# Low-rank products in couples of opposite row halves, and the key sums of a pair read one place later, in the projection stage of a two-layer backbone

## Chip, cores, metric

The kernel runs on 1 core of one Trainium2 chip. The metric is device microseconds of one execution of the whole program.

## What is computed

Two DeepNorm layers on 1024 latent and 256 context tokens of width 1024. Layer 0 projects all 1280 tokens once (`e_w_in`) and feeds four gated-linear-attention heads and eight RWKV-7 heads; layer 1 is an mLSTM block. The change is in what stands between the projection and the RWKV scan. There, for each of the two directions:

```python
p = p + (quad_shift(p, grid[0], grid[1]) - p) * mu
r, k, v, g, wl_f, wl_b, al_f, al_b = split_cols(p, RWKV_SIZES)
kk = to_heads(k * k_k, RWKV_HEADS).astype(jnp.float32)
kk = kk * lax.rsqrt(jnp.maximum(jnp.sum(jnp.square(kk), -1, keepdims=True), 1e-24))
w = jnp.exp(-RWKV_DECAY_SCALE * jax.nn.sigmoid((w0 + jnp.tanh(w_lr) @ ww2).astype(jnp.float32)))
a = jax.nn.sigmoid(a0 + a_lr @ wa2)
kh = to_heads(k * (1.0 + (a - 1.0) * k_a), RWKV_HEADS)
bonus = jnp.sum(rh * kh * rk, -1, keepdims=True) * vh
```

`w_lr` and `a_lr` have rank 64 per direction, so `w_lr @ ww2` and `a_lr @ wa2` contract over 64 rows only.

## The kernel before

**The projection stage** (`project_phase`) makes 26 column tiles of 128 channels, numbered as in `TILES0`: tile 0 is `wl` (the decays' low-rank channels, forward direction in rows 0 to 63 and backward in 64 to 127), tile 1 is `al` (the same for `a`), then k, r, v, g of head pairs 0 to 3 in tiles 2 to 17, then the linear-attention tiles 18 to 25. Each tile's 1280 tokens are cut into three pieces, `PIECES`, of 512, 512 and 256 columns. `project_split` (lines 469 to 471) runs 24 TensorE (PE) matmuls for a piece, since weights and activations are each split into a high and a low part.

**What is interleaved.** Beside the projection, the stage prepares the RWKV scan pair by pair. Pair p starts at tile b = 5 + 5p, so pairs 0 to 3 start at tiles 5, 10, 15 and 20. The table `PREP_PE` says which small products PE runs after which piece of which tile:

- `w0`, `a0` (forward low-rank products, three pieces each) after pieces 0 and 1 of tile b; `w1`, `a1` (backward) after pieces 0 and 1 of tile b+1 (line 869);
- `ksum`, the head sums of squared keys, three pieces against a full-height 128x128 constant, after piece 2 of tile b+1 (line 872);
- `blk0` after piece 1 of tile b+4, `blk1` and `bonus` of the pair before after pieces 1 and 2 of tile b (lines 857 and 872).

All of these write to two PSUM banks, 6 and 7, in turn. The product with number x in that order may start only when the product x-2 has been read:

```python
x = PREP_SEQ.index((name, p, i))
return x, 6 + x % 2
```

and `bank_free(x)` waits for `by_act` (ScalarE, ACT, read it) or `by_dve` (VectorE, DVE, read it).

**The other engines** work through the tiles in order, each with a `prep(n)` for the pair ahead of its own work on tile n:

- ACT: `high(n+1)` (the next tile's weights, line 911), `prep(n)` (sigmoids at k = n - b of 0 and 1, line 927; logarithm, root and the six exponentials at k = 2, lines 950 to 952 and 935 to 940), eviction of tile n (line 966), then `post(n-1)`.
- DVE: `prep(n)`, then the seven `shift_op`s that mix tile n (lines 487 and 495) once ACT has evicted it. At k = 1: squares (1039, 1040), `decay(p, 0)` and `decay(p, 1)` (ten scans, line 1008, and a subtraction, 1010, each; each waits for the third piece of `a0` or `a1`), then the three pieces of `ksum` are read out of PSUM (line 1047). At k = 2: kk times the root (1050). At k = 3 and 4: the operands of the scan. At k = 0 of the next pair: `blocks(p-1, 1)` (line 1018), which first waits until SyncE (SP) has stored the blocks of the forward direction, then the bonus (1032).
- SP issues all DMAs of the stage in one queue: weights, stored tiles, the scan's operands (`put`, line 764), and the block products (`blocks_away`, eight transfers, line 771).
- GpSimd (POOL) makes the low part of each tile's weights (line 980).

Of the kernel before, what the change touches and what calls it, by code (L numbers as in the profile page):

```python
# [22 lines left out]
P = 128  # L23
# [7 lines left out]
CH = 128  # L31
NCH = T // CH
# [124 lines left out]
NPAIR = len(PAIR_PARAMS)  # L157
# [64 lines left out]
def front_program(nc, A, G, xnat, hi, lo, w, wlr, win, modw, modb, modrow, gates_sb, full, rows, c_rows, cols1):  # L222
# [6 lines left out]
    n_rows = NPAIR + 1 + 2 + 1 + 2 * TILE_PARAMS  # L229
    sems = ("consts x_in c_in c_ps rows_in zeroed modb_in w0 w1 w2 w3 mod_k cols cols_sb cond_sb mod_ps mod_row vec_ps vec_sb gates_ps gate_row "  # L230
            "gate_ps gate_sb stored w_in small_in turned taken hi_ok lo_dve lo_pool")
    with phase(nc, sems) as (block, s):
# [100 lines left out]
        def _(act):  # L333
# [10 lines left out]
            act.dma_start(rows[V_MULR:V_MULR + 2, 0, :],  # L344
                          A.p["rwkv_mu"][0, 2048:2304].rearrange("(i n) -> i n", n=P)).then_inc(s["rows_in"], 16)
# [176 lines left out]
PREP_PE = {}  # L522
for _p in range(4):
    _b = PREP_AT + PREP_TILES * _p
    PREP_PE[_b, 0], PREP_PE[_b, 1] = [("w0", _p)], [("a0", _p)] + ([("blk1", _p - 1)] if _p else [])
    PREP_PE[_b, 2] = [("bonus", _p - 1)] if _p else []
    PREP_PE[_b + 1, 0], PREP_PE[_b + 1, 1], PREP_PE[_b + 1, 2] = [("w1", _p)], [("a1", _p)], [("ksum", _p)]
    PREP_PE[_b + 4, 1] = [("blk0", _p)]
PREP_PE[PREP_AT + 4 * PREP_TILES, 1] = [("blk1", 3)]
PREP_PE[PREP_AT + 4 * PREP_TILES, 2] = [("bonus", 3)]  # L530
PREP_SEQ = [(name, p, i) for key in sorted(PREP_PE) for name, p in PREP_PE[key] for i in range(2 if name[0:3] == "blk" else 3)]
# [11 lines left out]
def values_phase(nc, A, G, hi, lo, free, win, w, wh, wl, wvh, wvl, wlr):  # L543
# [8 lines left out]
    with phase(nc, sems) as (block, s):  # L552
# [6 lines left out]
        def _(sp):  # L559
# [17 lines left out]
            for n in range(2):  # L577
                sp.wait_ge(s["hi_ok"], 2 + n)
                sp.wait_ge(s["lo_pool"], 2 + n)
                sp.dma_start(w[:, n], win[:, :, TILES0[n][2]:TILES0[n][2] + P]).then_inc(w_in[n], 16)  # L580
# [8 lines left out]
            for i in range(2):  # L589
                sp.wait_ge(v_out[i], 16 * (NCH // 2))  # L590
                sp.wait_ge(w_in[i], 32)
# [88 lines left out]
def project_phase(nc, A, G, xnat, hi, lo, LW, LA):  # L680

    win = A.p["e_w_in"][0].rearrange("(k p) n -> p k n", p=P)
    with ExitStack() as ctx:
# [41 lines left out]

        def job(n):
# [7 lines left out]
        with phase(nc, sems) as (block, s):  # L734
# [26 lines left out]
            def _(sp):  # L761
# [12 lines left out]
                def load_wab(p):  # L774
                    if p:
                        sp.wait_ge(s["pp_ps"], PREP_SEQ.index(("a1", p - 1, 2)) + 1)
                    for d in range(2):
                        for i, x in enumerate(("rwkv_ww2_", "rwkv_wa2_")):
                            sp.dma_start(wab[64 * d:64 * d + 64, i], A.p[x + "fb"[d]][0][:, p * P:(p + 1) * P]).then_inc(s["lr_in"], 16)
# [58 lines left out]
            def _(pe):  # L838
# [8 lines left out]
                def block_product(p, d):  # L847

                    ops = (aa[0], sg[0]) if d == 0 else (sg[1], kk)
                    for h in range(2):  # L850
                        x, bank = piece_of(f"blk{d}", p, h)
                        bank_free(x)
                        q = slice(64 * h, 64 * h + 64)
                        for c in range(NCH):
                            for k in range(4):
                                t = slice(c * CH + 32 * k, c * CH + 32 * k + 32)
# [2880 lines left out]
```

## Time and profile before

| | us |
|---|---|
| median of 3 runs (lowest, highest) | 2911.9 (2903.33, 2916.92) |
| the profiled execution, its own time | 2909.42 |
| its span | 2907.6 |
| PE busy, share of span | 2505.9, 86% |
| DVE, ACT, POOL busy | 1625.3, 918.4, 786.4 |
| mean granted clock of PE, as a share | 0.922 |

The profile is one execution. The span runs from its first to its last instruction; 1.8 us lie around it. The projection stage's tiles begin at 169.9 us and its last product starts at 640.2 us. PE is busy 86% of the span as a mean over stages of quite different kinds, so the share says little about this stage; it is read by its own windows below. In the timelines, neighbouring records of one line on one engine are merged into a row, and what stands in brackets is the idle time before the row and what ended it. An fp32 matmul leaves two records.

### The profile page before, as it was taken

To read this page: it belongs to the slowest core of one execution; us is meant where nothing else is said; L and a number is where in the kernel's file an instruction comes from. 1 tells how busy PE (TensorE), PEld (TensorE's weight loads), DVE (VectorE), ACT (ScalarE), POOL (GpSimd) and SP (SyncE) were. 2 spreads that over 40 slices of the span, in tenths; PEclk is the share of its full clock that TensorE was granted. 3 is DMA by queue.
4 is the path that set the end of the run, shared out by engine and by line. 5 is a ranking of instruction groups with operands and counts; after the bars stand their busy time and mean duration, and the time that the engine had idled before them with its cause. 6 is when DMAs were issued, how large, how long until landed. Compare 5 with 4: busy or idle time off the path is not lost. (4 is left out here: it accounts for less than half of the span.)

```text
span 2907.6 us, 56618 instructions
## 1 busy us (share of the span) xinstructions
PE 2505.9 (86%) x24270; PEld 2129.0 (73%) x24270; DVE 1625.3 (56%) x2534; ACT 918.4 (32%) x1488; POOL 786.4 (27%) x745
## 2 busy tenths in 40 slices
PE   6899999987989884675978999999699999996986
PEld 2577776666877873554766888788599999996865
DVE  3037787644555635883585665665545656564233
ACT  2113243321232235552213333333343434340311
POOL 1111111107666533120313222222222222121421
PEclk8899999997999985777988999999899999998998
DMA  7612445644424413121562444444624343412521
GB/s 270 241 52 85 138 135 147 194 144 146 125 66 124 121 46 92 48 57 41 182 127 86 155 164 161 166 153 151 241 99 164 109 160 125 145 59 77 201 91 60
DMA packets 338281, 374.11 MB, mean 129 GB/s; under 512 B 111279, under 2 KB 274742, under 8 KB 335470
## 3 DMA queue, kind: packets, MB, share of 16 engines
q1 hardware_dynamic: 337024, 367.15, 39.2%
q8 instruction: 192, 3.15, 0.4%
q10 hardware_dynamic: 1006, 3.33, 0.3%
q14 instruction: 59, 0.48, 0.1%
HBM read 230.60 MB, written 139.82 MB: 127 GB/s over the span
## 5 line engine op out<-in xcount | busy, mean ns | idle before, releaser
L3321 PE MATMUL PS<-V_hi,weights_hi 128*128 128x258 f32 x832 | 237.8, 286 | 10.4 <-DVE H L3532 6.9
L469 PE MATMUL PS<-hT_hi,w_in_hi 128*128 128x512 f32 (+1 forms) x640 | 239.6, 374 | 4.7 <-DVE q_out L3120 4.7
L3322 PE MATMUL PS<-V_lo,weights_hi 128*128 128x258 f32 x832 | 236.7, 285 | 0.0
L471 PE MATMUL PS<-hT_hi,w_in_lo 128*128 128x512 f32 (+1 forms) x640 | 236.4, 369 | 0.0
L470 PE MATMUL PS<-hT_lo,w_in_hi 128*128 128x512 f32 (+1 forms) x640 | 236.3, 369 | 0.0
L3323 PE MATMUL PS<-V_hi,weights_lo 128*128 128x258 f32 x832 | 235.8, 283 | 0.0
L469 PE MATMUL PS<-h_hi,w_in_hi 128*128 128x512 f32 (+1 forms) x624 | 230.2, 369 | 5.6 <-PEq L115 3.6
L3429 POOL TENSOR_TENSOR weights_lo<-weights,weights_hi 128x1664 fp32r<-128x1664 f32 x32 | 122.0, 3813 | 412.6 <-ACT weights_hi L3381 412.6
L470 PE MATMUL PS<-h_lo,w_in_hi 128*128 128x512 f32 (+1 forms) x624 | 225.9, 362 | 0.0
L471 PE MATMUL PS<-h_hi,w_in_lo 128*128 128x512 f32 (+1 forms) x624 | 225.6, 362 | 0.0
L3293 PE MATMUL PS<-Q_hi,K_hi 128*128 128x256 f32 x640 | 184.7, 289 | 29.2 <-DMA K_lo<-kl_d 13.9
L3294 PE MATMUL PS<-Q_lo,K_hi 128*128 128x256 f32 x640 | 183.8, 287 | 0.0
L3295 PE MATMUL PS<-Q_hi,K_lo 128*128 128x256 f32 x640 | 183.7, 287 | 0.0
L980 POOL TENSOR_TENSOR w_in_lo<-w_in,w_in_hi 128x1024 fp32r<-128x1024 f32 x25 | 65.2, 2607 | 411.3 <-ACT w_in_hi L911 411.3
L3108 DVE SCALAR_TENSOR_TENSOR xnew<-padl,tile_cols,xnew 128x1024 f32<-128x1024 f32 x128 | 168.5, 1317 | 3.4
L3321 PEld LDWEIGHTS PS<-V_hi,weights_hi 128*128 128x128 f32 x832 | 158.6, 191 | 11.3 <-issue 11.3
L3322 PEld LDWEIGHTS PS<-V_lo,weights_hi 128*128 128x128 f32 x832 | 159.3, 191 | 0.0
L3323 PEld LDWEIGHTS PS<-V_hi,weights_lo 128*128 128x128 f32 x832 | 159.1, 191 | 0.0
L3367 ACT ACTIVATE weights<-M_row,head_cols 128x128 f32<-128x128 f32 x352 | 112.1, 389 | 114.1 <-DVE diag_arg L3477 58.5
L3293 PEld LDWEIGHTS PS<-Q_hi,K_hi 128*128 128x128 f32 x640 | 125.5, 196 | 30.7 <-issue 30.7
L469 PEld LDWEIGHTS PS<-hT_hi,w_in_hi 128*128 128x128 f32 x640 | 121.2, 189 | 33.3 <-DVE q_out L3120 13.6
L469 PEld LDWEIGHTS PS<-h_hi,w_in_hi 128*128 128x128 f32 x624 | 122.0, 195 | 26.4 <-issue 9.3
(462 smaller groups left out, 6348.6 us busy)
## 6 DMA issues: line engine op xcount, KB each, us to landing
chunk_in<-in_d SPq DMA_DIRECT2D x40, 512.0 KB, 3.4
w_in<-in_e_w_in_dram SPq DMA_DIRECT2D x30, 512.0 KB, 5.2
xnew<-in_o_w_in_dram SPq DMA_DIRECT2D x30, 512.0 KB, 6.2
in_d<-xnat SPq DMA_DIRECT2D x20, 640.0 KB, 6.0
modw<-in_mod_w_dram SPq DMA_DIRECT2D x12, 1024.0 KB, 9.5
xnat<-in_mod_w_dram SPq DMA_DIRECT2D x8, 1536.0 KB, 7.3
v_d<-xnew SPq DMA_DIRECT2D x16, 640.0 KB, 3.0
kh_d<-k_hi SPq DMA_DIRECT2D x16, 640.0 KB, 2.9
```

The source lines that it names most:

```text
L469: pe.matmul(PS[:, bank + off // 512, 0:n], wh[:, k], hh[:, k, t], start=(k == 0), stop=False)
L470: pe.matmul(PS[:, bank + off // 512, 0:n], wh[:, k], hl[:, k, t], start=False, stop=False)
L471: last = pe.matmul(PS[:, bank + off // 512, 0:n], wl[:, k], hh[:, k, t], start=False, stop=(k == KT - 1))
L3108: ins = dve.scalar_tensor_tensor(lat, padl[:, a:a + ROWS, b:b + GRID_W], col[tap], lat, ALU.mult, ALU.add)
L3293: pe.matmul(out, kh, QH[:, m % 2, kt], start=(kt == 0), stop=False)
L3294: pe.matmul(out, kh, QL[:, m % 2, kt], start=False, stop=False)
L3295: last = pe.matmul(out, kl, QH[:, m % 2, kt], start=False, stop=(kt == 3))
L3321: pe.matmul(out, wh, VH[:, j, q], start=(j == seen[0]), stop=False)
L3322: pe.matmul(out, wh, VL[:, j, q], start=False, stop=False)
L3323: last = pe.matmul(out, wl, VH[:, j, q], start=False, stop=(j == seen[-1]))
L3367: last = act.activation(W[:, n % 2, slot(d, c, j)], arg, ACT.Exp, bias=cols[:, d, j, h, 0:1], scale=-1.0)
L3429: pool.tensor_tensor(WL[n % 2][:], W[:, n % 2], WH[n % 2][:].bitcast(F32), ALU.subtract).then_inc(s["w_lo"], 1)
```

## The change

It has three parts. First, the channels of tile 1 (`al`) are loaded with their two 64-column halves exchanged, and so are its mix coefficients in the parameter rows, and `wa2` lies in the other half too. So `w` and `a` of one direction contract over opposite halves of the rows. This costs one more weight DMA for tile 1 (SP) and two more small parameter DMAs at the start (ACT). Second, `w` and `a` of a direction are issued as couples, piece by piece: one couple after each piece of tile b (forward) and of tile b+1 (backward). Third, `ksum` moves from after piece 2 of tile b+1 to after piece 0 of tile b+2; DVE reads it at k = 2 instead of k = 1, and kk times the root moves from k = 2 to k = 3.

The diff's core:

```diff
 for _p in range(4):
     _b = PREP_AT + PREP_TILES * _p
-    PREP_PE[_b, 0], PREP_PE[_b, 1] = [("w0", _p)], [("a0", _p)] + ([("blk1", _p - 1)] if _p else [])
...
+    for _d in range(2):
+        for _i in range(3):
+            PREP_PE[_b + _d, _i] = [(f"w{_d}", _p, _i), (f"a{_d}", _p, _i)]
+    if _p:
+        PREP_PE[_b, 1] += prep_all("blk1", _p - 1)
+        PREP_PE[_b, 2] += prep_all("bonus", _p - 1)
+    PREP_PE[_b + 2, 0] = prep_all("ksum", _p)
+    PREP_PE[_b + 4, 1] = prep_all("blk0", _p)
...
+        def half_of(i, d):
+
+            return d if i == 0 else 1 - d
...
+                            q = 64 * half_of(i, d)
+                            sp.dma_start(wab[q:q + 64, i], A.p[x + "fb"[d]][0][:, p * P:(p + 1) * P]).then_inc(s["lr_in"], 16)
...
+                    if name[0] in "wa":
+                        j = "wa".index(name[0])
+                        at = 64 * half_of(j, int(name[1]))
+                        q = slice(at, at + 64)
+                        ins = pe.matmul(PS[:, bank, 0:m], wab[q, j], (LW, LA)[j][q, t], start=True, stop=True)
...
-                    for name, dst, j in ((f"w{d}", sg[d], J_W0 + d), (f"a{d}", aa[d], J_A0 + d)):
-                        for i in range(3):
+                    for i in range(3):
+                        t, m = pieces(i)
+                        for name, dst, j in ((f"w{d}", sg[d], J_W0 + d), (f"a{d}", aa[d], J_A0 + d)):
...
                         decay(p, 0)
                         decay(p, 1)
+                    if k == 2:
                         for i in range(3):
                             x, bank = piece_of("ksum", p, i)
                             t, m = pieces(i)
                             dve.wait_ge(s["pp_ps"], x + 1)
                             dve.tensor_scalar(khs[:, t], PS[:, bank, 0:m], 1e-24, None, ALU.max).then_inc(s["by_dve"], 1)
-                    if k == 2:
+                    if k == 3:
                         dve.wait_ge(s["root"], p + 1)
                         link(dve.tensor_tensor(kk, kk, khs, ALU.mult))
-                    if k == 3:
                         dve.wait_ge(s["r_in"], 16 * (p + 1))
```

**The order on PE**, before, at tile 10 (`a0` of pair 1, `blk1` of pair 0, then the projection's piece 2) and, after the dots, at the end of tile 11 (`ksum` of pair 1):

```order
L471 MATMUL PS<-h_hi,w_in_lo 128x512
L869 MATMUL PS<-LA,w_pair_lr 128x512 x2
L869 MATMUL PS<-LA,w_pair_lr 128x256
L857 MATMUL PS<-pair_bufs,xnat 32x32 x80
L469 MATMUL PS<-h_hi,w_in_hi 128x256
...
L471 MATMUL PS<-h_hi,w_in_lo 128x256
L872 MATMUL PS<-pair_bufs,cst_pair 128x512 x2
L872 MATMUL PS<-pair_bufs,cst_pair 128x256
L469 MATMUL PS<-h_hi,w_in_hi 128x512
```

and with the change, the same places and the start of tile 12. `LW` and `LA` are tiles 0 and 1, the low-rank activations; lines 471 to 473 are the projection now, 889 the low-rank products, 877 the block products, 891 `ksum` and `bonus`:

```order
L473 MATMUL PS<-h_hi,w_in_lo 128x512
L889 MATMUL PS<-LW,w_pair_lr 128x512
L889 MATMUL PS<-LA,w_pair_lr 128x512
L877 MATMUL PS<-pair_bufs,xnat 32x32 x80
L471 MATMUL PS<-h_hi,w_in_hi 128x256
...
L889 MATMUL PS<-LW,w_pair_lr 128x256
L889 MATMUL PS<-LA,w_pair_lr 128x256
L891 MATMUL PS<-pair_bufs,cst_pair 128x512 x2
L891 MATMUL PS<-pair_bufs,cst_pair 128x256
...
L473 MATMUL PS<-h_hi,w_in_lo 128x512
L891 MATMUL PS<-pair_bufs,cst_pair 128x512 x2
L891 MATMUL PS<-pair_bufs,cst_pair 128x256
L471 MATMUL PS<-h_hi,w_in_hi 128x512
```

A run of three products of one kind became couples of `LW` and `LA` of one piece; the bonus now has a couple ahead of it; and the head sums have a tile's first piece ahead of them, 24 projection matmuls of 512 columns.

**The order on DVE**, before, pair 1: scans of the two directions, head sums, mix of tile 11, kk times the root:

```order
L1008 SCALAR_TENSOR_TENSOR xnat<-cst,xnat 128x128 x10
L1010 TENSOR_TENSOR xnat<-xnat 128x1280
L1008 SCALAR_TENSOR_TENSOR xnat<-cst,xnat 128x128 x10
L1010 TENSOR_TENSOR xnat<-xnat 128x1280
L1047 TENSOR_SCALAR pair_bufs<-PS 128x512 x2
L1047 TENSOR_SCALAR pair_bufs<-PS 128x256
L487 TENSOR_SCALAR p_out<-xnat,mix_keep 128x1280
L495 SCALAR_TENSOR_TENSOR p_out<-xnat,mix_mus,p_out 128x16x63 x2
L495 SCALAR_TENSOR_TENSOR p_out<-xnat,mix_mus,p_out 128x960 x2
L495 SCALAR_TENSOR_TENSOR p_out<-xnat,mix_mus,p_out 128x255 x2
L1050 TENSOR_TENSOR pair_bufs<-pair_bufs 128x1280
```

and with the change (1029 scans, 1031 subtraction, 489 and 497 the mix, 1069 head sums, 1072 kk times the root):

```order
L1029 SCALAR_TENSOR_TENSOR xnat<-cst,xnat 128x128 x10
L1031 TENSOR_TENSOR xnat<-xnat 128x1280
L1029 SCALAR_TENSOR_TENSOR xnat<-cst,xnat 128x128 x10
L1031 TENSOR_TENSOR xnat<-xnat 128x1280
L489 TENSOR_SCALAR p_out<-xnat,mix_keep 128x1280
L497 SCALAR_TENSOR_TENSOR p_out<-xnat,mix_mus,p_out 128x16x63 x2
L497 SCALAR_TENSOR_TENSOR p_out<-xnat,mix_mus,p_out 128x960 x2
L497 SCALAR_TENSOR_TENSOR p_out<-xnat,mix_mus,p_out 128x255 x2
L1069 TENSOR_SCALAR pair_bufs<-PS 128x512 x2
L1069 TENSOR_SCALAR pair_bufs<-PS 128x256
L489 TENSOR_SCALAR p_out<-xnat,mix_keep 128x1280
```

The three reads of the head sums stood ahead of the seven mix operations of tile 11 and now stand behind them; kk times the root went from ahead of the mix of tile 12 to behind it.

## Rows read from the trace of the kernel before

**Rows 1.** The page: busy time of TensorE (busy us, share, instructions).
```profile
PE 2505.9 (86%) x24270; PEld 2129.0 (73%) x24270; DVE 1625.3 (56%) x2534; ACT 918.4 (32%) x1488; POOL 786.4 (27%) x745
```

**Rows 2.** Windows: PE, PEld, DVE, ACT, POOL busy us (x instructions), clock, DMA share.
```profile
338.20:435.50 97.30, 91.95 (x719) 70.64 (x718) 78.32 (x82) 37.56 (x40) 11.78 (x5) 0.96 0.47 138
435.50:531.90 96.40, 91.33 (x718) 69.79 (x717) 80.99 (x87) 35.72 (x39) 13.53 (x6) 0.96 0.52 151
```

**Rows 3.** Groups of PE's small products: xcount | busy us, mean ns | idle before.
```profile
L869 PE MATMUL PS<-LW,w_pair_lr 64*128 64x512 f32 x32 | 15.8, 615 | 0.0
...
L872 PE MATMUL PS<-pair_bufs,cst_pair 128*128 128x256 f32 x16 | 6.0, 457 | 5.7 <-DVE pair_bufs L1047 5.7
L869 PE MATMUL PS<-LW,w_pair_lr 64*128 64x256 f32 x16 | 5.7, 438 | 5.0 <-ACT xnat L927 5.0
```

**Rows 4.** Timeline of PE, pair 1: start us, length us, line, records [idle before].
```profile
371.37 0.70 PE L869 MATMUL PS<-LW,w_pair_lr 64*128 64x256 f32 x2 [1.26 <-ACT xnat L927]
...
384.78 1.88 PE L872 MATMUL PS<-pair_bufs,cst_pair 128*128 128x512 f32 x4
387.87 0.70 PE L872 MATMUL PS<-pair_bufs,cst_pair 128*128 128x256 f32 x2 [1.21 <-DVE pair_bufs L1047]
```

**Rows 5.** Timeline of PE, later stage: products that alternate between row halves.
```profile
805.18 2.06 PE L1284 MATMUL PS<-chunk_in 64*128 64x128 f32 x32
```

**Rows 6.** Timeline of DVE, pair 1: scans, head sums taken, mix of tile 11.
```profile
382.42 3.27 DVE L1008 TENSOR_TENSOR_SCAN xnat<-cst,xnat 128x128 f32<-128x128 f32 x10 [3.06 <-ACT xnat L927]
385.72 1.49 DVE L1010 TENSOR_TENSOR xnat<-xnat 128x1280 f32<-128x1280 f32 x1
387.13 1.28 DVE L1047 TENSOR_SCALAR pair_bufs<-PS 128x512 f32<-128x512 f32 x2
...
388.94 1.35 DVE L487 TENSOR_SCALAR p_out<-xnat,mix_keep 128x1280 f32<-128x1280 f32 x1
390.33 6.12 DVE L495 SCALAR_TENSOR_TENSOR p_out<-xnat,mix_mus,p_out 128x1008 f32<-128x1008 f32 x6
```

**Rows 7.** Timeline of ACT, pair 1: last sigmoids, eviction, logarithm, last exponential.
```profile
381.30 1.09 ACT L927 ACTIVATE xnat<-PS,vc 128x512 f32<-128x512 f32 x2 [0.17 <-PE PS L869]
384.98 1.24 ACT L966 ACTIVATE xnat<-PS 128x1280 f32<-128x1280 f32 x1 [2.59 <-PE PS L471]
...
389.06 1.28 ACT L950 ACTIVATE pair_bufs<-pair_bufs 128x1280 f32<-128x1280 f32 x1 [0.60 <-DVE pair_bufs L1047]
...
399.32 1.35 ACT L940 ACTIVATE xnat<-xnat,half 128x1280 f32<-128x1280 f32 x1
```

**Rows 8.** Windows, columns as in rows 2: granted clock after two waits.
```profile
328.00:334.90 6.90, 6.12 (x30) 5.96 (x31) 6.73 (x9) 0.35 (x1) 0.00 (x0) 0.51 0.58 173
345.10:348.50 3.40, 3.40 (x10) 2.63 (x9) 3.29 (x4) 0.00 (x0) 0.00 (x0) 0.50 1.11 327
```

**Rows 9.** Timeline of PE: end of a block product of pair 0.
```profile
328.78 0.32 PE L857 MATMUL PS<-xnat 64*32 64x32 f32 x4 [2.96 <-issue]
```

**Rows 10.** Timeline of DVE: block products of pairs 0, 1, 2 taken.
```profile
355.15 1.09 DVE L1018 TENSOR_TENSOR blocks_out<-PS,cst_pair 128x320 f32<-128x320 f32 x2 [3.25 <-PE PS L857]
...
457.32 0.89 DVE L1018 TENSOR_TENSOR blocks_out<-PS,cst_pair 128x320 f32<-128x320 f32 x2 [3.37 <-DMA blk_d<-blocks_out]
...
552.78 0.89 DVE L1018 TENSOR_TENSOR blocks_out<-PS,cst_pair 128x320 f32<-128x320 f32 x2 [15.89 <-DMA blk_d<-blocks_out]
```

**Rows 11.** Timeline of PE: bonus products of pairs 0, 1, 2.
```profile
360.14 2.57 PE L872 MATMUL PS<-pair_bufs,cst_pair 128*128 128x512 f32 x6
...
457.96 3.97 PE L872 MATMUL PS<-pair_bufs,cst_pair 128*128 128x512 f32 x6 [2.35 <-DVE blocks_out L1018]
...
554.16 2.57 PE L872 MATMUL PS<-pair_bufs,cst_pair 128*128 128x512 f32 x6
```

**Rows 12.** Timeline of ACT's DMA issues and of PE, start of the program.
```profile
29.54 1.29 ACTq L355 DMA_DIRECT2D param_rows<-in_ml_skip_dram  x2
...
41.49 0.36 PE L316 MATMUL PS<-cst,param_rows 59*128 59x59 f32 x1
```

More of the change, by code:

```diff
@@ L522, with prep_all @@
 PREP_PE = {}
+def prep_all(name, p):
+    return [(name, p, i) for i in range(2 if name[0:3] == "blk" else 3)]
 for _p in range(4):
     _b = PREP_AT + PREP_TILES * _p
-    PREP_PE[_b, 0], PREP_PE[_b, 1] = [("w0", _p)], [("a0", _p)] + ([("blk1", _p - 1)] if _p else [])
[L526 to L531, printed above, removed]
+    for _d in range(2):
[6 more added lines that the diff above has]
+    PREP_PE[_b + 4, 1] = prep_all("blk0", _p)
+PREP_PE[PREP_AT + 4 * PREP_TILES, 1] = prep_all("blk1", 3)
+PREP_PE[PREP_AT + 4 * PREP_TILES, 2] = prep_all("bonus", 3)
+PREP_SEQ = [x for key in sorted(PREP_PE) for x in PREP_PE[key]]
 BY_ACT = [x for x in PREP_SEQ if x[0][0] in "wa"]
@@ L845, in bank_free, with block_product @@
                             pe.wait_ge(s["by_dve"], BY_DVE.index(before) + 1)
-                def block_product(p, d):
+                def block_product(p, d, h):
                     ops = (aa[0], sg[0]) if d == 0 else (sg[1], kk)
[L850 to L856, printed above, removed]
-                                ins = pe.matmul(PS[32 * k:32 * k + 32, bank, 32 * c:32 * c + 32], ops[0][q, t], ops[1][q, t],
-                                                start=True, stop=True)
-                        ins.then_inc(s["pp_ps"], 1)
@@ L861, in prep_product @@
[L861 to L873 removed]
+                    x, bank = piece_of(f"blk{d}", p, h)
@@ new lines, in block_product, with prep_product @@
+                    bank_free(x)
+                    q = slice(64 * h, 64 * h + 64)
+                    for c in range(NCH):
+                        for k in range(4):
+                            t = slice(c * CH + 32 * k, c * CH + 32 * k + 32)
+                            ins = pe.matmul(PS[32 * k:32 * k + 32, bank, 32 * c:32 * c + 32], ops[0][q, t], ops[1][q, t],
+                                            start=True, stop=True)
+                    ins.then_inc(s["pp_ps"], 1)
+                def prep_product(name, p, i):
+                    x, bank = piece_of(name, p, i)
+                    t, m = pieces(i)
+                    bank_free(x)
+                    if name[0] in "wa":
[3 more added lines that the diff above has]
+                        ins = pe.matmul(PS[:, bank, 0:m], wab[q, j], (LW, LA)[j][q, t], start=True, stop=True)
+                    else:
+                        ins = pe.matmul(PS[:, bank, 0:m], G.c("heads"), khs[:, t], start=True, stop=True)
+                    ins.then_inc(s["pp_ps"], 1)
@@ L884, in _ @@
                             ins.then_inc(s["prod"], 1)
-                        for name, p in PREP_PE.get((n, i), []):
-                            if name == "w0":
+                        for name, p, j in PREP_PE.get((n, i), []):
+                            if name == "w0" and j == 0:
                                 pe.wait_ge(s["lr_in"], 64 * (p + 1))
```

47 lines of the change are left out of this document (21 added, 26 removed).

## Prediction

> **What bounds the kernel now.** I read the page first: TensorE (PE) is busy for 2505.9 us, 86% of the span [rows 1], but that is a mean over many stages. The windows of the projection stage decide. While pairs 1 and 2 are prepared, PE is busy for 91.95 of 97.30 and for 91.33 of 96.40 us, VectorE (DVE) for 78.32 and 80.99, ScalarE (ACT) for some 36, and the DMA engines are about half busy [rows 2]. So PE sets the pace, and DVE follows with only about 17% to spare: PE time saved is worth its full length only while DVE, and what DVE releases, keeps up. The third view is the groups of PE's small products with their idle time, and the last is the timeline of one pair on each engine. I take pair 1: tile 11 ends at 384.78 us, where its head sums start. I call that moment E.
>
> **Low-rank products (removed PE time).** They take PE 15.8 + 5.7 us for `w` and as much for `a`, 43 in all, and 5.0 us of waiting for ACT to read the first of three pieces [rows 3]; without the last records' tails this is 47 us. A record of 512 columns costs 0.43 us: four took 1.88 us, of which 0.17 is a tail [rows 4]. A product is two records, so three pieces are 2.15 us, and the sixteen runs of three are 34.4 us. The other 7.6 us (47 less 34.4 and 5.0) are openings, two per run (one after the projection, one after the bank wait), 0.24 us each. Do two products in opposite row halves overlap? Before, no low-rank pair does, so I bound it. From below: 32 records of 64 rows and 128 columns, alternating between halves, took 2.06 us with their tail [rows 5]; one after another they would take a quarter of 0.43 us each, 3.4 us. Without the 0.27 us tail they ran at 1.8 us, so nearly two at a time. From above: no overlap, if a couple is too short. The rows have the same shape and kind of instruction, so I take full overlap. Then a couple costs one product: 8 x 2.15 = 17.2 us, and 24 openings x 0.24 = 5.7 us. **47 becomes 23: -24 us.** The bank wait of 1.26 us [rows 4] goes, since ACT now has a whole piece of projection to read a couple.
>
> **Clock.** After three of those waits PE's granted clock fell to 0.50 for 3.4 us (1.2 instead of 2.4 GHz) [rows 8], which show one. Each costs half of that: **-5 us.**
>
> The Trainium skill (TensorEngine Tiling, Key Properties) says that a change of tiling mode drains the engine. It speaks against couples, which change the mode 24 times instead of 16. It gives no price. By the rows this is the 0.24 us opening, already in the sum.
>
> **Head sums of squared keys.** Three products go to two banks, so the third waits until DVE has read the first. Before, DVE read it ahead of the mix of tile 11, and PE waited for 1.21 us in pair 1 [rows 4], 5.7 us in all [rows 3]. Now the read stands behind that mix, which cannot start before tile 11 is finished and evicted. In pair 1, from E: last couple 0.6, its two sigmoids 0.9 (512 and 256 columns took 1.09 [rows 7]), so the second scans can begin at 1.5. Scans 3.3 and subtraction 1.4: 6.2. Meanwhile the eviction (1.24 [rows 7]) is over at 2.8. The mix ran from 388.94 to 396.45, 7.5 us [rows 6]: 13.8. Reading the first piece, 0.7: 14.5. PE, after couple (0.6), a piece of projection (5.6) and two head sums (1.9), wants the bank at 8.2. It waits for **6.3 us**. Pair 2 has a mixed tile in the same place: 6.3 again. In pair 0 DVE is further behind; I take 8.5. In pair 3 the tile there is not mixed, the read is done at 6.9, and there is no wait. Together 21 us in place of 5.7: **+15.5 us.** A weight operation of GpSimd that holds up one DVE operation would add up to 2 us each; scans that have begun earlier would take off 1.
>
> **Clock after these waits.** A wait of 2.96 us [rows 9] was followed by 6.9 us at a clock of 0.51 [rows 8], a loss of 3.4. The shortest low stretch costs 1.7. I take 2.6 for each of three waits, less 1.7 that pair 0 pays already: **+6 us**, bounds +3 and +9.
>
> **What is late next.** DVE's last read of the sums at E + 16 releases ACT's logarithm. From there to the end of the last exponential ACT took 11.6 us (389.06 to 400.67) [rows 7], and the eviction of tile 12 stands behind it, so it comes at E + 29. Before, nothing held it. PE, itself 8 us late, has finished that tile at E + 25. kk times the root (1.5 us) now precedes the operands of the scan. Together DVE runs 3 to 5 us later against PE; I take 3. At tile 10, 15 and 20 a new couple stands ahead of the bonus, in a bank that DVE frees by reading the block product. PE also gets there 4.7 us earlier than before (3.9 and 2.9 us of low-rank work become 2.1). The gap closes by 7.7 us. Before, DVE had read the first half-block 4.5 us ahead of PE's bonus in pair 0 and 0.9 ahead in pair 2, and PE waited 2.35 in pair 1 [rows 10, 11]. So the added waits are 3.2, 7.7 and 6.8: **+17.5 us**, bounds 0 and +25.
>
> **The rest, at nothing.** Two more parameter DMAs on ACT, 0.65 us each: the last was issued by 30.8 us and PE uses them at 41.49 [rows 12]; with more than 12 us gone from that gap they would count. One more weight DMA on SP's queue, tile 1, issued a tile ahead of its use. `load_wab` issues four transfers as before, and SP passes no new wait. The order of ACT's sigmoids changes, not their number.
>
> **Sum:** -24 - 5 + 15.5 + 6 + 17.5 = +10 us. The profiled execution took 2909.42 us, 2.5 below the median of 2911.9: **2919 us**, 0.25% above the median. A measurement can tell about 0.5% from no change, 14.6 us, so this counts as no change. Most of what the couples save is paid back in waits for DVE.
>
> **Rivals.**
>
> *DVE's chain takes over (slower).* DVE has 78 to 81 us of work per pair [rows 2]. Add its new idle time behind ACT's exponentials (13 us, E + 16 to E + 29) and the waits for block stores (3.4 in pair 1 [rows 10]), for the bonus and for sigmoids (8), and a pair takes 103 us or more against 96 to 97. The place is the couple ahead of the bonus; it decides once the block stores land over 10 us after PE wants the bank. For: the stores already set DVE's read in pairs 1 and 2 [rows 10]. Against: in pair 0 there are 4.5 us of slack. Three pairs with 8 more each instead of the 3.3 of my sum: 2933.
>
> *Records of a couple run in order (near no change, or slower).* `w` first record, `w` second, `a` first, `a` second: then only the middle two overlap, and a couple costs three records instead of two. That is 8 x (0.43 + 0.43 + 0.21) = 8.6 us more, some of it hidden by the waits: 2926. The rows of the alternating stream fit this as well, since in a long stream each record finds a partner.
>
> The Trainium skill (TensorE: Matmul & The Clock Gate, The mechanism) has matmuls start and end in strict program order. By that rule a couple would cost the three records, and the sum would be 2928. No row here has an isolated couple.
>
> *The couple ahead of the bonus does not wait (small gain).* DVE catches up, having idle time before the next pair: 2902. For: two of three pairs had slack.
>
> *Neither wait comes (faster).* The head sums are read in time, so the savings of 29 us stay: 2881. Against it is the order on DVE, where the read follows the mix of a tile that PE has just finished.
>
> **How the numbers follow.** Forecast 0.50, DVE's chain 0.20, in order 0.12, no wait at the couple 0.13, neither wait 0.05. The forecast's own bounds are 2908 to 2929. The range for 8 in 10 leaves out the gain and the far end of the slow rival: 2899 to 2937. Slower by over 0.5% (above 2926.5): nearly all of the chain rival, half of the in-order rival, a seventh of the forecast, 0.32. Faster by over 0.5% (below 2897.3): 0.06. The rest: 0.62.
>
> **What would show it.** Low-rank products busy for 17 to 23 us instead of 43, two records starting together in each couple (in order: three record times). PE's third head sum idle for 6 to 9 us in pairs 0, 1 and 2, ended by DVE's read, none in pair 3. The mix of tile 12 starting about E + 30. A wait of 3 to 8 us at the third couple of tiles 10, 15 and 20, ended by DVE's read of the block product. The forecast is wrong if the head sums' wait stays under 3 us, or if the stage before tile 5 or anything behind the projection changes by more than 3 us.

## The result, and the profile of the changed kernel

The changed kernel takes 2927.1 us (median of 6 runs) beside 2914.1 us for the kernel before (6 runs in the same set). The ratio is 1.0057, with a 95% interval of 1.0039 to 1.0074: slower, by about the half per cent that a measurement of this kernel can tell from no change. The profiled execution spans 2922.9 us, 15.3 more than the one of before.

**Where the 15.3 us are.** The next stage's first product starts at 659.26 us before and at 672.25 now: 13.0 us come from the projection stage, 2.3 from everything behind it. Within the stage I add up PE's time on the timeline, from the first record of a group to the first record of the next (a wait counts with the group ahead of it), until the last bonus:

| PE time in the stage, us | before | change | difference |
|---|---|---|---|
| projection, with the waits at its groups' ends | 382.5 | 390.5 | +8.0 |
| low-rank products | 47.0 | 28.7 | -18.3 |
| head sums and bonus | 23.0 | 43.7 | +20.7 |
| block products | 17.8 | 20.7 | +2.9 |
| sum | 470.3 | 483.6 | +13.3 |

The page (busy us, share, instructions) answers to [rows 1]: PE does the same number of instructions in 11 us less, and the span is longer.

```profile
PE 2494.7 (85%) x24270; PEld 2127.6 (73%) x24270; DVE 1626.1 (56%) x2534; ACT 916.4 (31%) x1488; POOL 792.4 (27%) x745
```

Windows from the first couple of tile 10 to that of tile 15, and on to that of tile 20 (columns as in [rows 2], which answer to them). A pair now takes 103 us instead of 96 to 97. PE is busy for 86 to 89 us of it, and DVE has its 78 to 82 us of work as before:

```profile
344.40:447.07 102.67, 86.15 (x717) 67.55 (x717) 82.33 (x84) 37.91 (x40) 14.55 (x6) 0.95 0.49 141
447.07:550.29 103.22, 89.46 (x716) 69.45 (x716) 77.98 (x82) 34.07 (x37) 14.18 (x5) 0.92 0.47 135
```

What PE waits for in the stage (us in total, times, longest). Before, these waits for DVE were 5.7 for head sums and 3.5 for block products; now they are 37:

```profile
PE PS L891 <- DVE pair_bufs L1069: 25.9, 4, 8.4
PE PS L889 <- DVE blocks_out L1039: 10.9, 4, 5.3
PE PS L877 <- issue: 8.0, 2, 5.1
...
PE PS L877 <- ACT xnat L948: 2.6, 3, 0.9
```

**The couple works.** Timeline of PE in pair 1 (start, length, line, records, idle before), beside [rows 4]. The first records of `w` and `a` start 0.01 us apart, and so do the second ones, 0.53 us later. The couple of 512 columns, from its first record to the projection's next one, takes 1.06 us, the couple of 256 columns 0.63:

```profile
375.67 0.69 PE L889 MATMUL PS<-LW,w_pair_lr 64*128 64x512 f32 x1
375.68 0.69 PE L889 MATMUL PS<-LA,w_pair_lr 64*128 64x512 f32 x1
376.21 0.59 PE L889 MATMUL PS<-LW,w_pair_lr 64*128 64x512 f32 x1
376.21 0.59 PE L889 MATMUL PS<-LA,w_pair_lr 64*128 64x512 f32 x1
...
386.01 1.88 PE L891 MATMUL PS<-pair_bufs,cst_pair 128*128 128x512 f32 x4
396.08 1.22 PE L891 MATMUL PS<-pair_bufs,cst_pair 128*128 128x256 f32 x2 [8.19 <-DVE pair_bufs L1069]
```

**The head sums wait.** Timeline of DVE in pair 1, beside [rows 6]. E, the end of tile 11, is at 379.80. The second scans begin at E + 1.6 and take 5.4 us instead of the usual 3.3. Then come the subtraction and the whole mix of tile 11, and only at 395.34 is the first piece read. PE had wanted that bank since 387.9. Behind the read DVE idles for 12.8 us, because ACT has the logarithm and six exponentials ahead of the eviction of tile 12:

```profile
381.40 5.42 DVE L1029 TENSOR_TENSOR_SCAN xnat<-cst,xnat 128x128 f32<-128x128 f32 x10 [1.31 <-ACT xnat L948]
386.86 1.49 DVE L1031 TENSOR_TENSOR xnat<-xnat 128x1280 f32<-128x1280 f32 x1
388.27 0.88 DVE L489 TENSOR_SCALAR p_out<-xnat,mix_keep 128x1280 f32<-128x1280 f32 x1
389.18 6.12 DVE L497 SCALAR_TENSOR_TENSOR p_out<-xnat,mix_mus,p_out 128x1008 f32<-128x1008 f32 x6
395.34 1.29 DVE L1069 TENSOR_SCALAR pair_bufs<-PS 128x512 f32<-128x512 f32 x2
...
410.55 0.89 DVE L489 TENSOR_SCALAR p_out<-xnat,mix_keep 128x1280 f32<-128x1280 f32 x1 [12.78 <-ACT xnat L987]
```

The timeline of ACT shows the same chain: logarithm at 397.80 (before: 389.06), eviction of tile 12 at 409.30.

```profile
397.80 1.27 ACT L971 ACTIVATE pair_bufs<-pair_bufs 128x1280 f32<-128x1280 f32 x1 [13.05 <-DVE pair_bufs L1069]
...
409.30 1.21 ACT L987 ACTIVATE xnat<-PS 128x1280 f32<-128x1280 f32 x1
```

The 2.1 us that the scans took longer coincide with one operation of GpSimd, on its timeline; the scan that started at 383.64 ended at 386.20. By the Trainium skill (GPSIMD Engine Reference, Specifications) GpSimd and VectorE contend for their memory interface when a VectorE instruction has two inputs there; the trace agrees.

```profile
383.52 2.39 POOL L1001 TENSOR_TENSOR w_in_lo<-w_in,w_in_hi 128x1024 fp32r<-128x1024 f32 x1 [15.19 <-ACT w_in_hi L932]
```

**The waits for block products.** On DVE, the reads of the two directions' block products in pair 1, and the second one of pair 2, answer to [rows 10]:

```profile
446.45 0.87 DVE L1039 TENSOR_TENSOR blocks_out<-PS,cst_pair 128x320 f32<-128x320 f32 x2
466.11 0.89 DVE L1039 TENSOR_TENSOR blocks_out<-PS,cst_pair 128x320 f32<-128x320 f32 x2 [3.54 <-DMA blk_d<-blocks_out]
...
568.28 0.89 DVE L1039 TENSOR_TENSOR blocks_out<-PS,cst_pair 128x320 f32<-128x320 f32 x2 [11.05 <-DMA blk_d<-blocks_out]
```

On PE the same two reads each end a wait, at the first couple of tile 15 (a place that my prediction did not have) and at the third, ahead of the bonus:

```profile
447.07 1.19 PE L889 MATMUL PS<-LW,w_pair_lr 64*128 64x512 f32 x1 [5.33 <-DVE blocks_out L1039]
...
457.56 1.57 PE L877 MATMUL PS<-pair_bufs,xnat 64*32 64x32 f32 x160 [0.86 <-ACT xnat L948]
466.65 0.79 PE L889 MATMUL PS<-LW,w_pair_lr 64*128 64x256 f32 x1 [4.46 <-DVE blocks_out L1039]
```

Of the 5.33 us at the first couple, 2.0 are GpSimd's again: the last DVE operation ahead of the read took 3.51 us instead of 1.49, while GpSimd worked from 442.26 to 445.18. Before, its operation began when that read was under way (436.52 and 436.27), and held up what came behind it.

```profile
443.01 3.51 DVE L1088 TENSOR_TENSOR pair_bufs<-pair_bufs,xnat 128x1280 f32<-128x1280 f32 x1
```

**The clock behind the head sums' waits.** Windows of the stretches at half clock that follow the waits in pairs 0, 1 and 2 (columns as in [rows 2]). They last 10.2, 6.8 and 6.8 us, and PE is busy for 6.2, 3.3 and 3.9 us of them:

```profile
286.80:297.00 10.20, 6.15 (x15) 4.81 (x16) 4.88 (x7) 4.40 (x4) 0.00 (x0) 0.50 0.38 116
392.60:399.40 6.80, 3.32 (x8) 2.65 (x9) 4.31 (x7) 1.58 (x2) 0.00 (x0) 0.50 0.49 148
501.80:508.60 6.80, 3.88 (x9) 3.12 (x10) 3.78 (x6) 2.14 (x2) 0.00 (x0) 0.50 0.56 171
```

### The profile page after: what moved, and what is told of

Read it like the earlier page. It is cut to its first block and busy times, and to the rows that moved or that the text cites. A ratio compares the mean times of both kernels' runs of the same rounds, so it can differ in the third digit from the quotient of the medians.

```text
span 2922.9 us, 56624 instructions
## 1 busy us (share of the span) xinstructions
PE 2494.7 (85%) x24270; PEld 2127.6 (73%) x24270; DVE 1626.1 (56%) x2534; ACT 916.4 (31%) x1488; POOL 792.4 (27%) x745
## 5 line engine op out<-in xcount | busy, mean ns | idle before, releaser
L3342 PE MATMUL PS<-V_hi,weights_hi 128*128 128x258 f32 x832 | 237.8, 286 | 10.4 <-DVE H L3553 6.9
```

What stands on the lines that cost most here:

```text
L3342: pe.matmul(out, wh, VH[:, j, q], start=(j == seen[0]), stop=False)
```

## The experiments

Theory A is that of the prediction: PE loses its time where DVE reads a bank late, first because the read of the head sums stands behind a mix, and then because ACT's logarithm follows that read. Theory B is the rival "DVE's chain takes over": DVE bounds the stage anyway, and a wait taken away in one place comes back in another. The ratios below are to the kernel before, run on the same chip in the same set; its median was 2915.6 us in the set of e1 to e4, 2911.7 in that of e5 to e8 and 2912.5 in that of e9b to e12b. So kernels of different sets are compared by ratio, and 0.1% is 3 us. "Stage" is the start of the next stage in the profiled execution (659.3 before), and "waits" what PE waits there for DVE.

| | us | ratio (95%) | stage | waits |
|---|---|---|---|---|
| the change | 2927.1 | 1.0057 (1.0039 to 1.0074) | 672.3 | 37.1 |
| e1, read ahead of the mix | 2902.4 | 0.9954 (0.9938 to 0.9969) | 653.0 | 18.0 |
| e2, couples alone | 2917.1 | 1.0012 (0.9999 to 1.0025) | 666.8 | 29.6 |
| e3, head sums' move alone | 2929.5 | 1.0050 (1.0033 to 1.0067) | 678.8 | 21.8 |
| e4, couples in one row half | 2938.2 | 1.0075 (1.0056 to 1.0093) | 686.8 | 32.1 |
| e5, e1 and root early | 2900.2 | 0.9962 (0.9949 to 0.9975) | 647.9 | 14.3 |
| e6, e1 and stores first | 2891.1 | 0.9937 (0.9921 to 0.9953) | 644.5 | 13.3 |
| e7, e1 and eviction between | 2892.1 | 0.9934 (0.9923 to 0.9946) | 640.8 | 11.8 |
| e8, e5, e6 and e7 together | 2888.0 | 0.9922 (0.9910 to 0.9934) | 636.2 | 7.3 |
| e9b, before, with the edits of e6 and e7 | 2907.8 | 0.9985 (0.9972 to 0.9998) | 657.0 | 5.7 |
| e10b, the change with them | 2919.5 | 1.0028 (1.0017 to 1.0039) | 669.1 | 30.6 |
| e11b, e12b in one row half | 2898.9 | 0.9958 (0.9946 to 0.9970) | 647.0 | 5.0 |
| e12b, e1 with them | 2888.9 | 0.9921 (0.9905 to 0.9938) | 637.5 | 8.3 |

### e1: the read ahead of the mix

```diff
                         decay(p, 1)
-                    if k == 2:
                         for i in range(3):
                             x, bank = piece_of("ksum", p, i)
```

> The change, but DVE reads the head sums ahead of the mix of tile b+1 (k = 1) instead of behind it; PE's place of the product (after piece 0 of tile b+2) and all else as in the change. Theory A (PE loses its time waiting for a read that stands behind the mix, and the later waits ahead of the bonus come from the same late read through ACT's logarithm): the third head sum waits for 1 to 1.5 us instead of 8.2 in pairs 0 to 2, ACT's logarithm starts some 8 us earlier against PE, DVE idles for under 8 us ahead of the mix of tile 12 instead of 12.8, and most of the 10.9 us of waits for the block products goes: 2927 less 21 less 4 to 10 = 2896 to 2902. Theory B (DVE's chain is the bound and the head sums' wait only shows it): the waits for block products grow by what the head sums' wait loses, and the time stays within 5 us of the change's, 2922 to 2932.

The time is 2902.4, 0.4 us above what theory A expects and 20 us from theory B. The timelines of PE and DVE in pair 1 show the third head sum waiting for 1.1 us instead of 8.2, and DVE idle ahead of the mix of tile 12 for 5.9 us instead of 12.8:

```profile
383.96 0.70 PE L891 MATMUL PS<-pair_bufs,cst_pair 128*128 128x256 f32 x2 [1.11 <-DVE pair_bufs L1068]
```
```profile
384.69 0.42 DVE L1068 TENSOR_SCALAR pair_bufs<-PS 128x256 f32<-128x256 f32 x1 [0.19 <-PE PS L891]
...
397.98 0.89 DVE L489 TENSOR_SCALAR p_out<-xnat,mix_keep 128x1280 f32<-128x1280 f32 x1 [5.91 <-ACT xnat L987]
```

So moving one read across one mix is worth 25 us by the medians and 1.0%, some 30 us, by the ratios; 19.3 us lie in the stage. What theory A has wrong is the rest: of 10.9 us of waits for block products 10.4 stayed (9.1 at couples and 1.3 at the last bonus), and 4.3 came up for operands at the block products of tiles 9, 14 and 19, where PE now arrives earlier than DVE is ready. So 22.6 us of waits for head sums went and 19.1 us of waits for DVE in all: a sixth came back, as theory B says of the whole. One thing e1 leaves open: it takes 6.9 us off DVE's idle time in pair 1 together with PE's wait, so it doesn't say how much of the gain came over either. e10b below takes time off DVE's idle time alone.

### e2: couples alone, e3: the move alone

```diff
-    PREP_PE[_b + 2, 0] = prep_all("ksum", _p)
+    PREP_PE[_b + 1, 2] += prep_all("ksum", _p)
```

with the read at k = 1 and kk times the root at k = 2, as before (e2). And, on the kernel before (e3), with the read at k = 2 and the root at k = 3:

```diff
-    PREP_PE[_b + 1, 0], PREP_PE[_b + 1, 1], PREP_PE[_b + 1, 2] = [("w1", _p)], [("a1", _p)], [("ksum", _p)]
+    PREP_PE[_b + 1, 0], PREP_PE[_b + 1, 1], PREP_PE[_b + 2, 0] = [("w1", _p)], [("a1", _p)], [("ksum", _p)]
```

> Parts one and two of the change alone: couples, with the head sums where they were before, after piece 2 of tile b+1 and read at k = 1. Theory A: the head sums now stand right behind a couple, whose backward scans (3.3 us and a subtraction of 1.5) stand ahead of their read on DVE, so the third sum waits for 4 to 6 us in all four pairs (before: 1.2), a little less in total than the 25.9 of the change; the read is some 7 us earlier than in the change, and the waits for block products shrink. About 2927 less 6 less 0 to 8: 2913 to 2921. Theory B (DVE's chain is the bound): within 5 us of the change. If moving the sums were what costs the couples their whole gain: 2927 less 20, 2907 or below.

> Part three of the change alone, on the kernel before: runs of three low-rank products as before, head sums after piece 0 of tile b+2 and read behind the mix of tile b+1. Theory A: a1 is done 2 us later against E than with couples, so the wait is the same or longer from there on: PE wants the bank at E + 7.6 and DVE reads at E + 9 to 11 in pairs 1 and 2 (E the end of tile b+1), a wait of 2 to 3.5 us instead of 1.2, since before the scans begin 3 us ahead of E, not 1.6 behind it. With the later logarithm +6 to +15 on the kernel before: 2920 to 2929. If the cost of part three is the same with or without couples (25.9 less 5.7): +20, 2934.

e2 came out within what was expected: 2917.1, a tie with the kernel before. The timeline of PE in pair 1 shows why couples alone save nothing: the head sums now follow the last couple directly, and the backward scans stand between it and the read.

```profile
375.83 1.96 PE L891 MATMUL PS<-pair_bufs,cst_pair 128*128 128x512 f32 x4 [0.65 <-ACT xnat L948]
383.63 1.22 PE L891 MATMUL PS<-pair_bufs,cst_pair 128*128 128x256 f32 x2 [5.84 <-DVE pair_bufs L1068]
```

e3 is 0.5 us above its range, 2929.5: the wait is 4.8 us in pairs 1 and 2, not 2 to 3.5. DVE's timeline has the reason: the mix took 8.1 us for its six operations here instead of 6.1, and the read followed it. The 2.0 us are in the first of the six (3.28 us instead of 1.27), which ran beside an operation of GpSimd from 393.16 to 396.17.

```profile
388.33 3.27 DVE L1008 TENSOR_TENSOR_SCAN xnat<-cst,xnat 128x128 f32<-128x128 f32 x10 [4.54 <-ACT xnat L927]
...
393.95 8.13 DVE L495 SCALAR_TENSOR_TENSOR p_out<-xnat,mix_mus,p_out 128x1008 f32<-128x1008 f32 x6
402.12 1.29 DVE L1048 TENSOR_SCALAR pair_bufs<-PS 128x512 f32<-128x512 f32 x2
```

The parts don't add up (+2 and +14, together +13 us): put on top of e3, couples take 20 us off the low-rank products (49.0 to 28.7) and add 15 us of waits for DVE. Part three alone costs what the whole change costs. With the read ahead of the mix it pays on top of the couples: e1 is at 0.9954, e2 at 1.0012. Without couples that was not run.

### e4: couples that can't overlap

```diff
         def half_of(i, d):

-            return d if i == 0 else 1 - d
+            return d
```

and the same for the halves of tile 1's weights and mix coefficients.

> The change with w and a of a direction in the same row half, so that nothing of a couple can overlap; order, waits and number of DMAs as in the change. Theory A with overlap worth a whole product: a couple of 512 columns takes 1.9 us instead of 1.06, PE's busy part of the low-rank products goes from 22 to 39 us, and the waits for block products (10.9) take up to half of the difference: 2927 plus 8 to 17, 2935 to 2944. Rival (the overlap is worth nothing, since PE has the waits anyway): within 4 us of the change.

Timeline of PE in pair 1: the records of `a` start when those of `w` are through, and the couple takes 1.91 us (1.06 in the change), exactly one product of 0.85 more.

```profile
375.19 1.12 PE L889 MATMUL PS<-LW,w_pair_lr 64*128 64x512 f32 x2
376.16 1.02 PE L889 MATMUL PS<-LA,w_pair_lr 64*128 64x512 f32 x2
```

The time is 2938.2, inside the 2935 to 2944 of theory A. It is 11 us above the change by the medians but only 5 by the ratios, whose intervals overlap, while the stage ends 14.6 us later in the profile. So the overlap seems to be worth something even with PE waiting as much as it does, and less than its 17 us; e11b below tells this more clearly. The couple also shows that the 0.2 us of opening in a couple are paid once per couple, with one row half as with two.

### e5, e6, e7: what PE still waits for in e1

e5 puts kk times the root back to k = 2. e6 moves SP's stores of the forward block products ahead of the operands':

```diff
                         if p:
+                            blocks_away(p - 1, 0)
                             sp.wait_ge(s["kh_ok"], p)
                             sp.dma_start(K, A.v0_d[p - 1]).then_inc(s["v_in"], 16)
...
-                            blocks_away(p - 1, 0)
                             sp.wait_ge(s["by_dve"], BY_DVE.index(("bonus", p - 1, 2)) + 1)
```

e7 evicts tile b+2 in the middle of ACT's exponentials:

```diff
                     for d in range(2):
+                        if d == 1:
+                            evict(n)
                         act.wait_ge(s["c_ok"], 2 * p + d + 1)
```

> e1_read_first with kk times the root back at k = 2, where DVE idles for 5.9 us ahead of the mix of tile 12 (behind ACT's exponentials), instead of at k = 3, where the block product of tile 14 waits for what follows it. If DVE's lateness is what PE still waits for in e1 (4.3 us for the operands of the block products, 9.1 us for the read of block products ahead of couples): the 1.4 us waits at tile 14 go (4.3 to under 1) and the waits ahead of couples shrink by up to 1.5 each: 2902 less 4 to 8, 2894 to 2898. If PE's own work bounds the stage by now: no change, 2899 to 2905.

> e1_read_first with the eight stores of a pair's forward block products issued by SP ahead of the load of v and the four stores of the backward operands, instead of behind them. DVE may overwrite its buffer of block products only when these stores have landed: it idled for 2.7 and 3.2 us there at tiles 10 and 15, and PE waited 2.4 and 2.8 us for it at the third couple, right ahead of the bonus. Theory (the wait at the third couple is the wait for these stores): DVE reads blk1 without idling for a DMA, the third couple's waits fall under 0.5, and the next mix starts 2.5 us earlier: 2902 less 4 to 7, 2895 to 2898. Rival (it is DVE's lateness that sets the read, the stores only come last by a little): under 1 us less.

> e1_read_first with ACT's eviction of tile b+2 between the exponentials of the two directions instead of behind all of them. The tile's last product is done some 4 us before the last exponential. Theory (DVE's 5.9 us of idle time ahead of the mix of tile 12 are passed on to PE as waits at the block products of tiles 14 and 15): the mix starts 3 to 4 us earlier, and PE's waits of 4.3 us (operands) and 3.9 us (first couple of tile 15) go: 2902 less 6 to 12, 2890 to 2896. Rival (DVE catches up before anyone waits): within 2 us of e1.

> e1_read_first with the three edits of e5, e6 and e7 together. If their waits are different ones and PE is the bound behind them: of the 18 us that PE waits for DVE in e1 under 5 are left, and 2902 less 14 to 18 = 2884 to 2888, 0.9% under the kernel before, about what the couples were worth in PE time (24 + 5). If they are the same wait (DVE's chain per pair), no more than the best of the three: 2890 to 2896.

**e6.** In the change, SP's queue (its own timeline) issues the operands' stores first, the last three of them stretched over 7 us, and the eight block stores behind them:

```profile
450.59 4.94 SPq L784 DMA_DIRECT2D in_d<-pair_bufs  x2
455.57 1.91 SPq L784 DMA_DIRECT2D in_d<-xnat  x1
457.53 7.24 SPq L791 DMA_DIRECT2D blk_d<-blocks_out  x8
```

With them first, DVE's read of the backward block products (its timeline, pairs 0 and 1) idles for no DMA any more, and PE's third couple at tile 15 waits for 0.4 us instead of 2.8:

```profile
350.07 0.89 DVE L1039 TENSOR_TENSOR blocks_out<-PS,cst_pair 128x320 f32<-128x320 f32 x2
...
446.38 0.89 DVE L1039 TENSOR_TENSOR blocks_out<-PS,cst_pair 128x320 f32<-128x320 f32 x2
```
```profile
446.93 0.70 PE L889 MATMUL PS<-LW,w_pair_lr 64*128 64x256 f32 x2 [0.37 <-DVE blocks_out L1039]
```

So in e1 the wait at the third couple was the wait for these stores. The wait at the first couple of tile 15 rose from 3.9 to 5.3 us. By the ratios e6 is 0.17% under e1, 5 us, and its stage ends 8.5 us earlier.

**e7** is 0.20% under e1, 6 us, the lower end of its range, and its stage ends 12.2 us earlier. The 4.3 us of waits for operands went, and the wait at the first couple of tile 15 fell from 3.9 to 1.4 us, but the one at the third couple rose from 2.8 to 6.4. For e6 and e7 the intervals overlap with that of e1, so the gain of each alone rests on the stage in one profile.

**e5** missed: the 4.3 us of waits for operands went and the stage ends 5.1 us earlier in the profile, but the waits for block products rose by 0.6 and no gain shows in the time (0.9962 beside 0.9954, the intervals overlap).

**e8** has 7.3 us of waits for DVE left, not under 5, and is at 0.9922, 9 us under e1 and clear of its interval. Its median of 2888.0 touches the 2884 to 2888 that was expected, but that range was counted from e1's median in another set; by the ratios 14 to 18 us were not reached. The three edits remove partly the same waits, which is theory B's half of the truth: each alone takes 3.7, 4.7 and 6.2 us of waits off, together they take 10.7. In the time such a shortfall does not show, since 9 us is about what the three ratios add up to. The 4.0 us that PE waits at the third couple of tile 15 in e8 have no idle time of DVE for a DMA ahead of them: there DVE's own work sets the read.

### e9b to e12b: what the couples are worth

> The kernel before (runs of three, no couples, head sums in their old place) with the two edits of e6 and e7 alone: the stores of the block products first, the eviction of tile b+2 between the exponentials. What couples are worth once their read is in time is the distance from here to e12b. PE waits little for DVE in the kernel before (3.5 us for block products, 5.7 for head sums), so the two edits can take away at most the 3.5 and a low clock behind them: 0 to 5 us under the kernel before, 2907 to 2912. If instead the two edits carried e8 and the couples nothing: 2890 to 2895.

> The change with the two edits of e6 and e7, the read of the head sums still behind the mix. Theory (the head sums' wait is set by scans and mix between E and the read, which the edits don't touch): three waits of 8 us stay, the waits for block products (10.9 us) fall to 3 to 6: 2927 less 5 to 10, 2917 to 2922. If all of the change's loss was DVE's lateness: under 2905.

> e12b with w and a in the same row half, so that couples don't overlap. In the change this cost 7 to 11 us, part of it hidden by PE's waits for DVE. With those waits mostly gone the whole 17 us of PE time (16 x 0.85 and 8 x 0.43) should show, less the 4 us wait that is left at tile 15: 13 to 17 us above e12b, 2901 to 2906. Rival (DVE bounds the stage in e12b): under 6 us above it.

> e8 without its edit of kk times the root (which gave nothing alone in e5): the couples, head sums read ahead of the mix, stores first, eviction between. Within 2 us of e8: 2886 to 2890, 0.8% under the kernel before.

This set takes the stores and the eviction out of the question by giving both edits to all four. e9b, e10b and e12b came out in their ranges. From the kernel before (e9b, 2907.8) to couples with the head sums read in time (e12b, 2888.9) it is 18.9 us. With the read behind the mix (e10b) the same couples are 11.7 us slower than e9b: the place of one read makes a difference of 31 us (e10b less e12b). e11b splits the 18.9: without overlap 8.9 are there already, and the overlap gives 10.0. In the 8.9, 5.1 are PE's waits for ACT (5.8 us in e9b, 0.7 in e11b). They also hold the move of the head sums, which wait for 2.2 us in e11b and 5.7 in e9b; this set does not separate it from the couples.

e10b also answers what e1 leaves open. In pair 1 DVE's idle time is 11.1 us instead of 12.8 ahead of the mix of tile 12, and nothing instead of 3.5 for the stores, 5.2 us less in all. The waits for block products fell from 10.9 to 4.7 us. Yet the head sums wait for 25.9 us as before, and the gain over the change is 0.29%, 8 us. So time taken off DVE's idle stretches did not move the wait for head sums, and the place of the read did. PE's and DVE's timelines in e10b:

```profile
396.73 1.22 PE L891 MATMUL PS<-pair_bufs,cst_pair 128*128 128x256 f32 x2 [8.18 <-DVE pair_bufs L1076]
```
```profile
409.53 0.89 DVE L489 TENSOR_SCALAR p_out<-xnat,mix_keep 128x1280 f32<-128x1280 f32 x1 [11.12 <-ACT xnat L958]
```

The 10.0 miss my 13 to 17, and the trace has two reasons. At tiles 10, 15 and 20 the second couple is followed directly by the block product and the third by the bonus, which wait until ACT has read the couple's banks. From the couple's start to theirs it is 1.99 and 1.35 us in both kernels, so 3 x 0.85 + 3 x 0.43 = 3.8 us of overlap are worth nothing there. Of the other 13.2, waits for DVE take 3.3 (8.3 instead of 5.0), of which 2.2 are at the third couple of tile 15 (3.7 instead of 1.5). That leaves 9.9. The agreement is closer than the sum deserves: waits labelled "issue" differ by 1.3 us too (8.7 and 7.4).

The windows of pairs 1 and 2 in e12b: 89 and 92 us per pair, in place of 103, with the clock at 1.00 and 0.98. On ACT's timeline the eviction of tile 12 now stands between the exponentials, and on DVE's the mix of tile 12 starts 2.3 us behind that of tile 11.

```profile
334.45:423.31 88.86, 84.04 (x718) 66.10 (x717) 79.40 (x84) 38.01 (x40) 12.94 (x5) 1.00 0.52 154
423.31:515.08 91.77, 85.86 (x716) 67.24 (x716) 80.95 (x83) 34.20 (x37) 13.81 (x6) 0.98 0.55 158
```
```profile
385.81 1.35 ACT L979 ACTIVATE xnat<-xnat,half 128x1280 f32<-128x1280 f32 x1
387.29 1.24 ACT L958 ACTIVATE xnat<-PS 128x1280 f32<-128x1280 f32 x1
388.43 1.36 ACT L974 ACTIVATE pair_bufs<-xnat,half 128x1280 f32<-128x1280 f32 x1
```
```profile
388.62 0.89 DVE L489 TENSOR_SCALAR p_out<-xnat,mix_keep 128x1280 f32<-128x1280 f32 x1 [2.28 <-ACT xnat L958]
```

e12b and e8 are both faster than either kernel of this case: 0.9921 (0.9905 to 0.9938) of the kernel before.

## Why the prediction was right, and where it was not

The forecast was "no change, leaning to slower, because waits for DVE pay back what the couples save": +7 on the median, measured +13, inside the range. That the late read of the head sums pays back what the couples save is shown by e1 and by e12b against e10b. Term by term:

- **Low-rank products, -24.** The couples themselves came out as forecast: 16 x 1.06 + 8 x 0.63 = 22.0 us, against 22.9. Full overlap was the right choice; a couple in order would have cost 1.06 + 0.43 = 1.49. But the change in this kind of work is -18.3, not -24. The step that failed is "the bank wait goes, since ACT now has a whole piece of projection to read a couple". That holds for 18 of 24 couples. The second and third couple at tiles 10, 15 and 20 have a block product or a bonus right behind them, and these wait for ACT's reads: the couples there take 1.99 and at least 1.35 us instead of 1.06 and 0.63, some 5 us, as much as the bank waits of before.
- **Rule of the Trainium skill on order.** The rule that I weighed (TensorE: Matmul & The Clock Gate, The mechanism: matmuls start and end in strict program order) would, as I read it, have given a third record time per couple. I had applied it to the records, both of `w` and then both of `a`. The trace has them start in the order `w`, `a`, `w`, `a` (375.67, 375.68, 376.21, 376.21), and the couple takes two record times. Between the two products the order holds: `w` starts and ends 0.01 us ahead of `a`, and that does not keep two row halves from working at once. The order in which the records were issued is in no row, so the rule itself is not refuted, only my price for it. The drain at a change of mode, which the Trainium skill states (TensorEngine Tiling (Array Packing), Key Properties), is at most the 0.2 us of opening per couple, and e4 has the same 0.2 us.
- **Head sums, +15.5.** Measured +20.2: 8.4, 8.2 and 8.2 us of wait in pairs 0 to 2, 1.1 in pair 3, against 8.5, 6.3, 6.3 and 0. The missing 2 us in pairs 1 and 2 are the operation of GpSimd that I named and left out of the sum; it fell into the scans in both.
- **Clock, -5 + 6.** Both parts came out, and nearly cancel. The three stretches of 3.4 us at half clock behind the waits for ACT are gone, 5 us. Behind the head sums' waits PE is busy at half clock for 13.4 us in pairs 0 to 2, where it was for 3.4 before (pair 0); half of the 10 more is 5 us. In the projection hardly anything is left of either: of its +8.0 all but 0.6 are waits (10.9 for block products now, 3.5 before).
- **Waits at the third couple, +17.5.** The term of the sum that was furthest off: 0.5, 4.5 and 0.7 us. With the 2.35 of before in pair 1, that is 0.5, 2.1 and 0.7 more, 3.3 in place of the 3.2, 7.7 and 6.8 of the forecast. My step was "the gap closes by 7.7 us" with a fixed DVE. In pair 2 DVE idles for 11 us ahead of that read (16 before), because tiles 18 and 19 are not mixed: DVE had room there to make up for being late, which a fixed lateness leaves out. What I didn't have is the wait of 5.3 us at the first couple of tile 15, for the forward block product: before, DVE read that one 0.8 us ahead of PE, and any lateness of DVE had to show there. All waits for block products together are +7.4 (10.9 less the 3.5 of before).
- **Not in the sum:** the waits labelled "issue" ahead of block products, 5.2 us before and 8.0 now.
- **What is late next** held: logarithm 8.7 us later, mix of tile 12 at E + 30.8 (forecast E + 30), DVE idle for 12.8 us (forecast 13).

The net is right to 3 us in the stage, and that is luck: a term that was 10 too high (block products) met two that were each 5 too low (low-rank products, head sums) and one that was absent (issue, 3). Of the rivals, "DVE's chain takes over" (2933) had the pair's time right: 103 us, and pairs 1 and 2 took 102.7 and 103.2. It had the place wrong, since PE's largest waits are at the head sums and not at the couple ahead of the bonus (0.5 to 4.5 us, not over 10). That a wait taken away comes back elsewhere, e1 refutes for five sixths of it, and in e10b less idle time of DVE left the head sums' waits as they were. For the last sixth it holds, and the edits of e5 to e7 together removed less waiting than their sum. "Neither wait comes" (2881) names the gain that was there to be had, and e8 and e12b got most of it by two edits on other engines.

## What to carry to other kernels

When a consumer's read of a shared bank is moved, look at what stands ahead of it on its own engine before looking at the producer: here the same product at the same place cost 8 us per pair behind a mix, and 1 ahead of it. Two half-height products in opposite row halves overlapped fully here, even as an isolated couple, but the time was saved only where nothing that needs a read of their banks was queued right behind them. And more of a saving on the engine that sets the pace is kept when the follower's own idle times (here behind ACT's exponentials and behind stores at the end of a queue) are shortened with it: e12b is at 0.9921, e1 at 0.9954.

## What the runs showed of the hardware

The stage behind the projection has the same instructions in the same order in all these kernels, and yet took from 449.5 us (e2) to 460.9 (e8) in the profiled executions, with a granted clock of PE between 0.94 and 0.91. The windows of that stage in e2 and in e8, in this order:

```profile
666.80:1116.30 449.50, 381.95 (x6856) 337.41 (x6856) 242.56 (x533) 127.28 (x284) 274.40 (x499) 0.94 0.34 99
```
```profile
636.20:1097.10 460.90, 392.75 (x6856) 348.34 (x6857) 240.52 (x533) 127.27 (x284) 274.74 (x499) 0.91 0.33 96
```

That is as much as most effects in this case, so a single profile can't rank two of these kernels by span (e3's span, 2921.2, is under the change's, though its stage ends 6.5 us later), and the start of the next stage is the better ruler for an edit within a stage. Whether the clock is granted by chance there or depends on where the stage before ends was not tried.

The waits labelled "issue" at the block products of tiles 9 and 20 took 5.2 and 5.4 us in all in the kernel before and in e9b, 6.8 in e3, and 6.4 to 9.8 in the kernels with couples. Their cause stays open.
